# Expert units of a two-layer decoder trunk: 21 units of mixed lists instead of 25, five sets of weights instead of four

## The reference

```python
def hierarchical_moe(xn, w_rg, b_rg, w_re, b_re, w1, w3, w2):
    g_prob = softmax(xt @ w_rg + b_rg)                 # 4 groups, the best one is taken
    e_logit = (xt @ w_re + b_re).reshape(T, 4, 8)      # 8 experts in a group, the best 2 are taken
    gate = p_g * top_p / sum(top_p)
    ...
    hid = silu(xb @ w1[e]) * (xb @ w3[e])              # 1024 -> 256
    ybuf = hid @ w2[e]                                 # 256 -> 1024
    y[token] += ybuf * gate
```

## Time and profile before

| | |
|---|---|
| median of 3 runs | 2068.63 us (2066.73 to 2073.2) |
| the profiled execution | 2067.3 us, span 2065.2 us |
| PE busy | 1913.7 us (93%) |
| DVE, ACT, POOL busy | 732.2, 566.0, 343.2 us |
| granted clock of PE | 0.967 of full speed on average |
| moved by DMA | 322.35 MB, 156 GB/s on average |

### The profile page before, as it was taken

One profiled execution on the slowest core, in us unless ns is written; L12 is line 12 of the kernel. 1 busy time (PEld: TensorE's weight loads), 2 busy tenths in 40 slices (PEclk: granted clock), 3 DMA queues, 4 the chain that ended last, 5 costly groups with the idle time before them and its releaser, 6 DMA issues. The chain is left out here.

```text
span 2065.2 us, 25615 instructions
## 1 busy us (share of the span) xinstructions
PE 1913.7 (93%) x9312; PEld 1095.1 (53%) x9312; DVE 732.2 (35%) x2115; ACT 566.0 (27%) x1337; POOL 343.2 (17%) x388
## 2 busy tenths in 40 slices
PE   7999998999899799999699999899998998999992
PEld 4555556767555444444355555477674554444441
DVE  0111116676444332221221221266773443222214
ACT  1211226655322111111121211455562221111110
POOL 0333331021000111111013333211100001111110
PEclk9999999999999899999799999999999997999996
DMA  7000010020171389999722110000206115999976
GB/s 254 11 21 11 0 51 1 2 83 12 44 290 69 126 329 409 400 402 370 264 85 78 41 52 21 31 2 2 93 2 246 64 57 205 370 404 405 395 292 254
DMA packets 94635, 322.35 MB, mean 156 GB/s; under 512 B 22065, under 2 KB 36017, under 8 KB 78129
## 3 DMA queue, kind: packets, MB, share of 16 engines
q1 hardware_dynamic: 70704, 271.92, 34.4%
q0 software_dynamic: 14400, 33.58, 4.2%
q10 hardware_dynamic: 9408, 15.23, 2.1%
HBM read 296.56 MB, written 42.99 MB: 164 GB/s over the span
## 5 line engine op out<-in xcount | busy, mean ns | idle before, releaser
L426 PE MATMUL banks<-r_win,r_tile 128*128 128x384 f32 (+3 forms) x1536 | 530.7, 504 | 9.9 <-DMA r_win<-in_w_in 7.6
L426 PEld LDWEIGHTS banks<-r_win,r_tile 128*128 128x128 f32 x1536 | 292.4, 192 | 227.0 <-issue 61.2
L1625 PE MATMUL banks<-r_proj,r_tile 128*128 128x512 f32 x512 | 236.3, 603 | 0.0
L1774 PE MATMUL banks<-r_proj 128*128 128x512 f32 x512 | 225.0, 592 | 0.0
L1096 ACT ACTIVATE r_win<-r_win 128x256 f32<-128x256 f32 (+7 forms) x256 | 177.3, 695 | 28.5 <-DVE r_win L1168 20.7
L979 PE MATMUL banks<-r_win 64*128 64x512 f32 (+3 forms) x704 | 135.0, 503 | 19.6 <-DVE r_win L1140 10.3
L1774 PEld LDWEIGHTS banks<-r_proj 128*128 128x128 f32 x512 | 94.8, 190 | 107.1 <-issue 107.1
L1774 PE MATMUL banks<-r_win,r_proj 128*64 128x512 f32 (+1 forms) x512 | 132.8, 610 | 10.1 <-DMA r_win<-in_w 5.9
L1625 PEld LDWEIGHTS banks<-r_proj,r_tile 128*128 128x128 f32 x512 | 92.4, 191 | 92.8 <-issue 92.5
L2127 DVE SCALAR_TENSOR_TENSOR r_proj<-banks,rs,r_proj 128x256 f32<-128x256 f32 x50 | 24.2, 484 | 326.4 <-ACT r_proj L1868 326.4
L990 PE MATMUL banks<-fixed,r_win 128*128 128x128 f32 x984 | 132.4, 280 | 7.2 <-ACT r_win L1104 7.1
(11 more groups left out here) (222 smaller groups left out, 2039.9 us busy)
## 6 DMA issues: line engine op xcount, KB each, us to landing
r_win<-in_w SPq DMA_DIRECT2D x96, 1024.0 KB, 14.2
r_proj<-in_w SPq DMA_DIRECT2D x96, 1024.0 KB, 14.8
r_win<-in_w_in SPq DMA_DIRECT2D x6, 1536.0 KB, 20.1
r_proj<-in_w_o SPq DMA_DIRECT2D x2, 4096.0 KB, 14.2
residual<-r_tile ACTq DMA_DIRECT2D x16, 512.0 KB, 3.0
out<-r_tile SPq DMA_DIRECT2D x16, 512.0 KB, 7.6
r_win<-expert_rows SPq DMA_DIRECT2D x16, 512.0 KB, 10.7
r_proj<-expert_rows SPq DMA_DIRECT2D x16, 384.0 KB, 3.6
```

The lines of the kernel that those rows point to most:

```text
L426: mm = pe.matmul(bk[b][:, 0:CHUNKS[c]], uT[j][:, k, :], w_ch[c][:, k, :], start=(k == 0), stop=(k == KT - 1))
L1625: mm = pe.matmul(bk[2 * (t % 2) + c][:, :], mix[t][:, k, :], s.w_o[:, k, 512 * c:512 * c + 512], start=(k == 0), stop=(k == KT - 1))
L1774: mm = pe.matmul(bk[2 + j][at, 0:2 * F].rearrange("p (c n) -> p c n", c=2), xT[j][:, k, at], w13[c][:, :, k, :], start=(k == 0), stop=(k = ...
```

## The change

The units are 21. Two hold one expert each, as before (ranks 0 and 1, 128 slots). Sixteen are mixed: 96 slots for one of ranks 2 to 17, and 32 slots for half of the list of one of ranks 18 to 25, whose other half lies in the next mixed unit. Three hold two experts of 64 slots (ranks 26 to 31). A mixed unit is multiplied in four parts of 32 columns, three with the long list's weights and one with the short one's. The order has the shared units at positions 10, 17 and 18; unit 18 holds ranks 30 and 31, and units 19 and 20 are the last two.

A fifth set of weights is added: in the first layer in `r_tile`, whose residual rows have been stored by then, in the second in `r_win`, which holds no input weights there. It is loaded first (rank 18), as soon as the expert numbers are there. The plan decides which expert goes into which set, and after which unit. The 27 loads of experts behind units are, from unit 0 on: 1, 1, 1, 2, 1, 2, 1, 2, 1, 2, 2, 1, 2, 1, 2, 1, 2, 2, and none behind the last three.

`rank_slots` makes its table with five small matmuls instead of three. The limit that decides on another pass is 96 slots, and one DVE step is added to the ranking.

```diff
-FULL, AT_ONCE = 18, 4
+ALONE, FULL, AT_ONCE = 2, 18, 4
+QUARTER, LONG = 32, 96
 FIRST_KEY = 2.0 ** 18
+SETS = 5
+SHARED_AFTER = (3, 6, 6)
...
+        self.col, self.ranks, self.slots = col, ranks, slots
 def plan_units(experts_n):
-    shared = (experts_n - FULL) // 2
-    singles = [3 * (f // 2) + f % 2 for f in range(FULL)]
-    units = [Unit(col, [c]) for c, col in enumerate(singles[:AT_ONCE])]
-    for i in range(shared):
-        units.append(Unit(3 * i + 2, [0, 1]))
-        units += [Unit(singles[AT_ONCE + 2 * i + c], [2 + c]) for c in range(2)]
-    used = [0] * 4
+    triples = (FULL - ALONE) // 2
+    units = [Unit(f, [f], [[(0, P)]]) for f in range(ALONE)]
+    quarters = [(q, q + QUARTER) for q in range(0, P, QUARTER)]
+    shared = FULL + triples
+    for i in range(triples):
+        for n in range(2):
+            f = ALONE + 2 * i + n
+            units.append(Unit(f, [f, FULL + i], [quarters[:3], quarters[3:]]))
+        for i_, after in enumerate(SHARED_AFTER):
+            if after == i:
+                units.append(Unit(FULL + i_, [shared + 2 * i_, shared + 2 * i_ + 1], [[(0, HD)], [(HD, P)]]))
+    assert shared + 2 * len(SHARED_AFTER) == experts_n
+    needed = []
     for u in units:
-        u.use = [used[c] for c in u.sets]
-        for c in u.sets:
-            used[c] += 1
-    return units
+        needed += [r for r in u.ranks if r not in needed]
+    needed = list(range(AT_ONCE)) + [r for r in needed if r >= AT_ONCE]
+    left_by = {r: max(n for n, u in enumerate(units) if r in u.ranks) for r in needed}
+    place = {r: (c, 0) for c, r in enumerate(needed[:SETS])}
+    first_loads, todo = [(c, r) for c, r in enumerate(needed[:SETS])], needed[SETS:]
+    for n, u in enumerate(units):
+        u.sets, u.loads = [place[r] for r in u.ranks], []
+        for r in u.ranks:
+            if left_by[r] == n and todo:
+                c, use = place[r]
+                place[todo[0]] = (c, use + 1)
+                u.loads.append((c, todo.pop(0)))
+    assert not todo
+    assert all(c >= 2 for u in units[-2:] for c, _ in u.sets)
+    return units, first_loads
...
-def weight_sets(s):
+def weight_sets(s, last_layer):
     n = s.KT * 2 * s.F + s.F // P * s.D
     at = s.KT * s.coff[-1] + s.KT * CHUNKS[-1] - 2 * n
-    assert at >= s.KT * s.coff[2]
-    return [s.r_win[:, at:at + n], s.r_win[:, at + n:at + 2 * n], s.r_proj[:, 15104:15104 + n], s.r_proj[:, 0:n]]
-CHOICE_STEPS, PLACE_STEPS, GATE_STEPS, RANK_STEPS = 14, 6, 6, 7
+    assert at >= s.KT * s.coff[2] and at >= n
+    return [s.r_win[:, at:at + n], s.r_win[:, at + n:at + 2 * n], s.r_proj[:, 15104:15104 + n], s.r_proj[:, 0:n],
+            s.r_win[:, at - n:at] if last_layer else s.r_tile[:, 8 * s.D - n:8 * s.D]]
+CHOICE_STEPS, PLACE_STEPS, GATE_STEPS, RANK_STEPS = 14, 6, 6, 8
...
-        eng.reg_mov(s.rounds[eng.engine], eng.value_load(s.nrounds[0:1, 0:1], min_val=1, max_val=NT))
+        eng.reg_mov(s.rounds[eng.engine], eng.value_load(s.nrounds[0:1, 0:1], min_val=1, max_val=-(-NT * P // LONG)))
...
-                for c in range(AT_ONCE):
+                for c, e in first_loads[:AT_ONCE]:
                     if c == 3:
                         sp.wait_ge(g.h.sem, g.h.at(layer, NT))
-                    load_w13(c, c)
-                    load_w2(c, c)
+                    load_w13(c, e)
+                    load_w2(c, e)
                 sp.wait_ge(g.id.sem, g.id.at(layer, 1))
+                if not last_layer:
+                    sp.wait_ge(g.hs.sem, g.hs.at(layer, 16 * NT))
+                for c, r in first_loads[AT_ONCE:]:
+                    e = expert(r)
+                    load_w13(c, e)
+                    load_w2(c, e)
                 left = []
                 for n in range(U):
-                    taken = [(c, expert(r)) for c, r in following(n)]
+                    taken = [(c, expert(r)) for c, r in units[n].loads]
...
-                to = bank[:, E * c:E * c + 27].rearrange("p (a b) -> p a b", b=3)
-                at = E * block
-                pe.matmul(to[:, :, 0:2], slots_t[rows, :],
-                          rank_of[rows, at:at + FULL].rearrange("p (a b) -> p a b", b=2), start=True, stop=True)
-                halves = rank_of[rows, at + FULL:at + FULL + 18].rearrange("p (a h) -> p h a", h=2)
+                to, of = bank[:, E * c:E * c + U], rank_of[rows, E * block:E * block + E]
+                pe.matmul(to[:, 0:FULL], slots_t[rows, :], of[:, 0:FULL], start=True, stop=True)
+                beside = to[P - QUARTER:P, ALONE:FULL].rearrange("p (a n) -> p n a", n=2)
+                shared = FULL + (FULL - ALONE) // 2
+                for n in range(2):
+                    pe.matmul(beside[:, n, :], slots_t[rows, QUARTER * n:QUARTER * (n + 1)], of[:, FULL:shared],
+                              start=True, stop=True)
+                halves = of[:, shared:E].rearrange("p (a h) -> p h a", h=2)
                 for h in range(2):
-                    mm = pe.matmul(to[HD * h:HD * (h + 1), :, 2], slots_t[rows, 0:HD], halves[:, h, :],
+                    mm = pe.matmul(to[HD * h:HD * (h + 1), FULL:U], slots_t[rows, 0:HD], halves[:, h, :],
...
-            pe.wait_ge(g.rk.sem, g.rk.at(layer, RANK_STEPS))
+            pe.wait_ge(g.rk.sem, g.rk.at(layer, RANK_STEPS - 2))
             pe.wait_ge(g.t0.sem, g.t0.at(layer, 1))
             rank_rows().then_inc(g.p0.sem, 1)
             pe.matmul(bk[4][0:1, 0:E], s.expert_col[0:2 * E, :], rank_of[0:2 * E, 0:E], start=True, stop=True)
             pe.matmul(bk[4][0:1, E:2 * E], count_of[0:2 * E, :], rank_of[0:2 * E, 0:E], start=True, stop=True)
+            pe.wait_ge(g.rk.sem, g.rk.at(layer, RANK_STEPS))
...
-                    if u.pair:
-                        return [(slice(HD * h, HD * (h + 1)), c) for h, c in enumerate(u.sets)]
-                    return [(slice(0, P), u.sets[0])]
+                    return [(slice(a, b), c) for (c, _), blocks in zip(u.sets, u.slots) for a, b in blocks]
                 def hidden(n):
                     u, j = units[n], n % 2
-                    for c, use in zip(u.sets, u.use):
+                    for c, use in u.sets:
...
-                step(v.tensor_scalar(limit, rank, float(FULL), float(HD), ALU.is_lt, ALU.mult))
+                link(v.tensor_scalar(alone, rank, float(ALONE), None, ALU.is_lt))
+                step(v.scalar_tensor_tensor(out=limit, in0=rank, scalar=float(FULL), in1=alone, op0=ALU.is_lt,
+                                            op1=ALU.add))
...
-            v.tensor_copy(limits, bk[4][:, 2 * E:3 * E])
+            v.tensor_scalar(limits, bk[4][:, 2 * E:3 * E], float(QUARTER), None, ALU.mult)
             v.tensor_reduce(cnt[0:1, 0:1], bk[4][0:1, E:E + FULL], AX.X, ALU.max).then_inc(g.nr.sem, 1)
             dve.wait_ge(g.nr.sem, g.nr.at(layer, 1))
-            v.scalar_tensor_tensor(out=cnt[0:1, 1:2], in0=bk[4][0:1, E + FULL:E + FULL + 1], scalar=2.0,
+            v.scalar_tensor_tensor(out=cnt[0:1, 1:2], in0=bk[4][0:1, E + FULL:E + FULL + 1], scalar=LONG / HD,
                                    in1=cnt[0:1, 0:1], op0=ALU.mult, op1=ALU.max).then_inc(g.nr.sem, 1)
             dve.wait_ge(g.nr.sem, g.nr.at(layer, 2))
-            v.tensor_scalar(cnti[0:1, :], cnt[0:1, 1:2], float(P - 1), None, ALU.add).then_inc(g.nr.sem, 1)
+            v.tensor_scalar(cnti[0:1, :], cnt[0:1, 1:2], 1.3333, float(P - 1), ALU.mult, ALU.add).then_inc(g.nr.sem, 1)
```

41 lines of the change are left out of this document (16 added, 25 removed).

## The result

The changed kernel takes **2032.41 us** (median of four runs, 2031.01 to 2035.27) against 2067.68 (2066.4 to 2073.2): ratio 0.9826, 95% interval 0.9805 to 0.9848. It is 1.7% faster. The forecast was 0.9%: right in sign, inside the range, but half the size. The profiled execution has a span of 2029.9 us.

What follows compares the result with a forecast made beforehand. Transfers, already 1.7 us a cycle slower than PE, were to set the pace. 2067.3 − 10.2 (second layer) − 8.1 (first) = 2049.0, with the median 1.3 above: 2050 us, 0.9% faster, range 2028 to 2068.

Steps and rivals of the forecast that it cites:

- Transfers set the pace: Expert stages: 1.6 experts loaded per unit take 14.9 us of transfer against 12.3 of PE, so PE must wait.
- PE's saving, 38 us a layer: Expert stages: four plain slots fewer save 46.5 us, twelve more shared units cost 8.0; net 38 per layer.
- Four parts cost what two halves cost: Mixed units: four 32-column parts cost no more than two halves, 12.3 us a unit, hidden product 7.0 to 7.3.
- Rival C: Mixed units: four parts don't pack, 3.1 us more in each of sixteen; slower, 2093 us; chance 9%.
- Start +3.5 us: Stage start: gather 0 shares the DMA with the fifth set's three pieces, so tokens arrive 3.5 us later (0 to 5).
- Hidden 3: Unit 3's hidden product in the second layer, predicted to end at 1766.7 instead of 1762.7.
- A piece costs 3.1 us: Weight loads: 1024 KB of one expert's w1, w3 or w2 takes 3.1 us (3.05 to 3.15), from 402 GB/s.
- The pivot: Unit 18 (ranks 30 and 31), waiting for its w3, piece 73: predicted at 1968.8 in the second layer.
- tail: From unit 18's start to the end of the last rows in the second layer: 44.6 us, ending at 2013.4.
- Fifth set, 9.3 us of early work: Stage start: three pieces issued at about 1713.6 instead of 1730.5 do 9.3 us of transfers in idle time.
- Rival A: Expert stages: PE sets the pace, needing pieces of 2.6 us; 1995 us in all; chance 5%.
- Rival B: Expert stages: no gain, the slowest part of a transfer falls up to 15 us behind; 2062 to 2070; chance 14%.

Runs made afterwards that it cites:

- its floor: Changed kernel with half loads of w1 and w3 in the second layer's unit loop: 2007.8 us, its second stage 269.7 us.
- The moved slots: Kernel before, two of eight hidden products per unit left out, with half of its 18 whole units starting their list at slot 64: 2024.6 us against 2047.7.
- late: Changed kernel with the fifth set loaded behind unit 0's hidden layer instead of once expert numbers are known: 2025.98 us, ratio 0.9802.
- 25 units with six of eight: Kernel before (25 units, four sets) with two of the eight hidden products of each unit left out: 2047.7 us, ratio 0.9899.

## Why the prediction was half right

**Transfers set the pace: right.** PE idles in the middle and stands 21 us above its floor. **PE's saving, 38 us a layer: right** within a tenth: 35.5.

**Four parts cost what two halves cost: right.** Predicted hidden product 7.0 to 7.3 us, measured 7.07, where the same view shows 7.03 for a full-width product and 7.09 for halves; removing the parts changes a stage by 1 us. A mixed unit's slot was to take 12.3 us and takes 12.25 (hidden products that start at 1744.20 and 1756.45). By the ratios of the Trainium skill that the prediction weighed ("TensorE: Matmul & The Clock Gate", Part 3: Packing small matmuls), 8.95 us had been due, an estimate; the measurement decides for the row of halves. Rival C is out.

**Start +3.5 us: right**, 3.6 and 3.2 us of waiting for gather 0 in the first and second layer. Hidden 3 was to end 53.3 us after the first gather (1713.42 to 1766.7), and did (1697.94 to 1751.28).

**A piece costs 3.1 us: this step failed.** I took 402 GB/s at share 1.00 for the ceiling, because share 1.00 reads as full. For 25 units that was nearly so: with PE out of the way they reach 405. What failed is that I carried the rate over to 21 units, because the bytes stay the same ("the bytes don't change: 28 experts, 84 pieces, 260 us per layer"); where the rows lie changed, and with it the rate. At 420 GB/s, of which the weight queue moved 88.09 of 104.51 MB, a piece takes 2.96 us. The pivot was to start 202.1 us after hidden 3 and started 194.8 after: 7.3 us too many, and 62 pieces of 0.14 us are 8.7. With a tail of 42.5 us for 44.6, those 7.3 are the missing 9.4 us of the second stage (19.6 against 10.2); the first missed 7.0 (15.1 against 8.1). The gathers and scatters of four units more had been loading the engines of the low slots: an estimate from the code is 25 x 2 x 8 slots x 4 KB, 1.64 MB beside the 5.5 MB of weights that each engine moves in a stage (88.09 / 16), and 1.38 MB with 21 units, 3.7% less on the fullest engine. With transfers alone setting the pace the rate rose from 405 to 419 GB/s, 3.5%. The moved slots show that such unevenness costs rate (405 to 421 GB/s with nothing else changed). That it is all of the difference between 25 and 21 units is argued from these sizes and from the stretches above, and no run moved the rows of 21 units back.

**Fifth set, 9.3 us of early work: failed too, without harm to the sum.** I listed it as a source of gain, yet had written that nearly all the first eleven pieces have landed by hidden 3; then it can't matter when the first three went. It was worth nothing, and its 3.5 us of price were paid in each layer: late, the load saves 6 us in all.

**The signs.** Waits of 20 to 30 us a layer for weights were forecast, some 15 came, since pieces were faster; they lie at units 11, 12, 17 and 18, as said. DMA share 1.00 at 400 to 410 GB/s was wrong. Rival A asked for pieces of 2.6 us; the truth lay a third of the way to it. Rival B wanted the slowest part further behind. It isn't: the widest spread of a w2 load's completions in the second stage is 19.5 us before and 18.5 in the changed kernel.

## What to carry to other kernels

A DMA share of 1.00 is no ceiling; look at how GB/s compares with the best of the kernel's stretches (422 and then 386 in one stage here), and at whether the spread between the engines' completions grows. When gathers skip empty slots and the transfers set the pace, spread the empty ones over all 128 partitions: in the 25 units with six of eight it cost two small products and gave 4% of rate and 23 us. Where PE stands right behind it gives next to nothing (4 to 6 us). And before adding a buffer to load earlier, ask when the load after it may go; if that is tied to a buffer coming free, early bytes are only moved about, and they can stand in the way of what the start waits for.

## What the runs showed that I had not expected

- Rows of a gather are tied to engines by slot: 384 GB/s with the high half of the slots empty, 421 with the odd half, though the first moves more rows (10.66 and 8.45 MB).
- Share and rate part company: 1.00 with 402 GB/s, 1.02 with 420. In the records of single packets the usual packet of 8192 B took 309 ns in both kernels, which is 424 GB/s on 16 engines; in the kernel before 3.1% of them took over 1.3 times that, in the changed one 0.6% (1770 to 1920 us).
- Four products of 32 columns run side by side at 512 moving columns: 7.07 us for 64 of them where 16 full-width ones took 7.03.
- Uneven rows cost no rate at first: 422 GB/s for the first part of a stage, while the engines drift up to 19 us apart, and 386 after that.
